# A hybrid decoder layer on one core: which expert's weights lie in the scratch's spare room

## The reference, cut to what matters

```python
logits = (xt @ w_router) + b_router
top_val, top_idx = lax.top_k(logits, 4)          # of 32 experts
gates = jax.nn.softmax(top_val, axis=-1)
hh = xb @ w_gu[e] + b_gu[e]                      # (tokens, 1024) @ (1024, 2048)
act = glu * jax.nn.sigmoid(1.702 * glu) * (lin + 1.0)
out += (act @ w_down[e] + b_down[e]) * gate      # (tokens, 1024) @ (1024, 1024)
```

## Time and profile before

| what | value |
|---|---|
| median of the runs | 1191.43 us |
| the profiled execution | 1193.07 us |
| its span, first to last instruction | 1191.3 us |
| around the span | 1.8 us |
| TensorE busy | 1137.9 us, 96% of the span |
| granted clock, mean | 0.997 |
| read from HBM | 433.04 MB |

### The profile page before, as it was taken

How to read it: one execution, slowest core, us unless ns; L and a number is a source line. 1 busy time by engine, 2 the same in 40 slices (tenths; PEclk the granted TensorE clock), 3 DMA queues, 4 the chain that set the end, 5 groups by cost and what they waited for, 6 DMA issues and landing times.

```text
span 1191.3 us, 16910 instructions
## 1 busy us (share of the span) xinstructions
PE 1137.9 (96%) x7060; PEld 482.3 (40%) x7060; DVE 282.8 (24%) x576; ACT 173.0 (15%) x319; POOL 0.2 (0%) x4
## 2 busy tenths in 40 slices
PE   7999999999999999999999999999999999999997
PEld 6888856533333333333333333333333333333234
DVE  2454734322111111112112111111111111111123
ACT  3323423110100000000100100000000000000015
POOL 0000000000000000000000000000000000000000
PEclk9999999999999999999999999999999999999999
DMA  9752026679899999999999999999999999999970
GB/s 367 328 212 74 30 116 239 247 298 415 348 418 427 429 426 429 430 429 427 430 428 427 430 429 427 430 429 427 429 429 427 428 430 427 429 429 427 429 329 35
DMA packets 34022, 434.67 MB, mean 365 GB/s; under 512 B 4032, under 2 KB 4288, under 8 KB 6976
## 3 DMA queue, kind: packets, MB, share of 16 engines
q1 hardware_dynamic: 33984, 434.11, 87.0%
HBM read 433.04 MB, written 1.05 MB: 364 GB/s over the span
## 4 chain that ended last, share of the span: by engine, by line
PE 44%; DMA 39%; DVE 1%; issue 0%; ACT 0%; SPq 0%; DVEq 0%
DMA ring<-in_we 38%; PE PS L909 30%; PE PS L1006 2%; PE PS L747 2%; PE PS L860 2%; PE PS L875 2%; PE PS L925 1%; PE PS L867 1%; PE PS L959 1%; DMA hT<-in_wproj 0%; PE PS L797 0%; PE PS L934 0%; PE PS L542 0%; PE PS L802 0%; PE PS L883 0%
## 5 line engine op out<-in xcount | busy, mean ns | idle before, releaser
L909 PE MATMUL PS<-ring,FV 128*64 128x512 f32 x2276 | 508.7, 596 | 22.6 <-DMA ring<-in_we 22.6
L909 PEld LDWEIGHTS PS<-ring,FV 128*64 128x64 f32 x2276 | 156.7, 137 | 355.4 <-issue 302.4
L909 PE MATMUL PS<-B,FV 128*64 128x512 f32 x772 | 175.1, 596 | 8.7 <-DMA B<-in_we 8.7
L909 PEld LDWEIGHTS PS<-B,FV 128*64 128x64 f32 x772 | 53.3, 137 | 115.6 <-issue 99.2
L530 PE MATMUL PS<-hT,ring 128*128 128x256 f32 x416 | 93.0, 382 | 1.0 <-ACT hT L1059 0.7
L530 PEld LDWEIGHTS PS<-hT,ring 128*128 128x128 f32 x416 | 78.3, 190 | 12.1 <-ACT hT L1059 0.9
L1540 DVE TENSOR_SCALAR rz<-con,lora 128x64 f32<-128x64 f32 x30 | 7.6, 255 | 304.5 <-PE PS L909 304.5
L1313 DVE TENSOR_TENSOR FV<-PS,prm 128x512 f32<-128x512 f32 x32 | 22.1, 692 | 184.4 <-PE PS L867 184.4
L1622 DVE TENSOR_SCALAR hT<-PS 128x512 f32<-128x512 f32 x32 | 22.1, 692 | 182.2 <-PE PS L909 182.2
L860 PE MATMUL PS<-xq,rz 128*64 128x512 f32 x256 | 62.0, 605 | 0.0
L1218 ACT ACTIVATE FV<-PS 128x512 f32<-128x512 f32 x32 | 19.1, 597 | 294.8 <-PE PS L959 294.8
(11 more groups left out here) (270 smaller groups left out, 686.2 us busy)
## 6 DMA issues: line engine op xcount, KB each, us to landing
ring<-in_we SPq DMA_DIRECT2D x135, 2048.0 KB, 23.4
B<-in_we SPq DMA_DIRECT2D x48, 2048.0 KB, 29.3
ring<-in_wz SPq DMA_DIRECT2D x7, 2048.0 KB, 23.2
ring<-in_we SPq DMA_DIRECT2D x14, 1024.0 KB, 7.3
ring<-in_wo SPq DMA_DIRECT2D x2, 2048.0 KB, 8.3
ring<-in_wgate SPq DMA_DIRECT2D x2, 2048.0 KB, 38.6
stash<-in_we SPq DMA_DIRECT2D x1, 2048.0 KB, 13.6
xq<-in_x SPq DMA_DIRECT2D x2, 512.0 KB, 6.0
```

The costliest lines, as they stand in the source:

```text
L909: mm = pe.matmul(PS[64 * h:64 * h + 64, bank_, :], lhs(4 * (q % 2) + k), early[u] if q == 0 and u < units else w[:, k, h, :], start=(first ...
```

## The change

The 14 units of scratch room take item 11's p1 and the first six units of item 11's p0 instead of item 3's. They are loaded at the same places in the attention part, from expert 11's weights. Item 3 is loaded in full by `ahead`, like its neighbours. In SP's order item 11's p0 is two units (512 KB) and its p1 is left out, and the wait and the two `wproj` DMAs come behind item 11's pieces, with the threshold 67 instead of 19. TensorE has item 11 written out, since it reads other rooms: items 0 to 3, a loop for items 4 to 9, items 10 and 11, a loop for items 12 to 29, and the last two. The kept piece has a semaphore of its own, so the thresholds of p1 change with it: `behind=True` marks the items after item 11, which wait for one landing of p1 less.

```diff
-        NEARLY, EARLY_ITEM = len(early), 3
+        NEARLY, KEPT_ITEM = len(early), 11
...
+        s_kept = sem("kept_item_second_piece_landed")
...
-            sp.dma_start(kept, t["we"][EARLY_ITEM, 1]).then_inc(s_we[1], 16)
+            sp.dma_start(kept, t["we"][KEPT_ITEM, 1]).then_inc(s_kept, 16)
...
-                sp.dma_start(dst, t["we"][EARLY_ITEM, 0, :, u * PW:(u + n) * PW]).then_inc(s_early, 16)
+                sp.dma_start(dst, t["we"][KEPT_ITEM, 0, :, u * PW:(u + n) * PW]).then_inc(s_early, 16)
...
-            def in_turn(i, odd, qs=range(6)):
+                    load(e if q < 3 else e_next, q, odd == (q < 3))
+
+            def in_turn(i, odd, qs=range(6), kept_item=False):
 
                 e = weights(i)
                 for q in qs:
+                    if kept_item and q == 1:
+                        continue
                     sp.wait_ge(s_used, 6 * i + (q - 5 if q < 3 else q - 11))
-                    load(e, q, odd)
+                    if kept_item and q == 0:
+                        sp.dma_start(ring[:, 0, NEARLY * PW:], t["we"][KEPT_ITEM, 0, :, NEARLY * PW:]).then_inc(s_we[0], 16)
+                    else:
+                        load(e, q, odd)
 
             ahead(2, False, halved=True)
-            ahead(EARLY_ITEM, True, rest=True)
-            sp.wait_ge(s_used, 6 * EARLY_ITEM + 1)
-            for k in range(2):
-                sp.dma_start(wproj1[k], t["wproj"][1, :, k * PW:(k + 1) * PW]).then_inc(s_ple1, 16)
+            ahead(3, True)
             with sp.Fori(1, EARLY) as p:
                 ahead(2 * p + 2, False)
                 ahead(2 * p + 3, True)
             in_turn(2 * EARLY + 2, False, range(3))
-            in_turn(2 * EARLY + 3, True)
+            in_turn(KEPT_ITEM, True, kept_item=True)
+            sp.wait_ge(s_used, 6 * KEPT_ITEM + 1)
+            for k in range(2):
+                sp.dma_start(wproj1[k], t["wproj"][1, :, k * PW:(k + 1) * PW]).then_inc(s_ple1, 16)
             with sp.Fori(EARLY, pairs) as p:
...
-            item(2, False, before=True)
-            item(EARLY_ITEM, True, units=NEARLY)
-            with pe.Fori(1, pairs) as p:
+            item(2, False)
+            item(3, True)
+            with pe.Fori(1, KEPT_ITEM // 2 - 1) as p:
                 item(2 * p + 2, False)
                 item(2 * p + 3, True)
-            item(2 * last_pair, False)
+            item(KEPT_ITEM - 1, False)
+            item(KEPT_ITEM, True, kept_item=True)
+            with pe.Fori(KEPT_ITEM // 2, pairs) as p:
+                item(2 * p + 2, False, behind=True)
+                item(2 * p + 3, True, behind=True)
+            item(2 * last_pair, False, behind=True)
             last_item = 2 * last_pair + 1
-            item(last_item, True, last=True)
+            item(last_item, True, last=True, behind=True)
```

More of the change, by code:

```diff
@@ L270, in fox_rwkv7_moe_ple @@
         s_odd = [sem(f"odd_expert_piece{q}_landed") for q in range(3, 6)]
-        s_early = sem("fourth_item_first_rows_landed")
+        s_early = sem("kept_item_first_rows_landed")
+        s_kept = sem("kept_item_second_piece_landed")
         s_ple = sem("layer_projection_landed")
@@ L431, in load, with ahead @@
                     .then_inc(landed(q, odd), 16)
-            def ahead(i, odd, rest=False, halved=False):
+            def ahead(i, odd, halved=False):
                 e, e_next = weights(i), weights(i, 1)
@@ L441, in ahead @@
                         continue
-                    if rest and q == 1:
-                        continue
                     sp.wait_ge(s_used, 6 * i + (q - 5))
[L445 to L448, removed]
-            def in_turn(i, odd, qs=range(6)):
+                    load(e if q < 3 else e_next, q, odd == (q < 3))
+            def in_turn(i, odd, qs=range(6), kept_item=False):
                 e = weights(i)
                 for q in qs:
+                    if kept_item and q == 1:
+                        continue
                     sp.wait_ge(s_used, 6 * i + (q - 5 if q < 3 else q - 11))
-                    load(e, q, odd)
+                    if kept_item and q == 0:
+                        sp.dma_start(ring[:, 0, NEARLY * PW:], t["we"][KEPT_ITEM, 0, :, NEARLY * PW:]).then_inc(s_we[0], 16)
+                    else:
+                        load(e, q, odd)
             ahead(2, False, halved=True)
-            ahead(EARLY_ITEM, True, rest=True)
-            sp.wait_ge(s_used, 6 * EARLY_ITEM + 1)
-            for k in range(2):
-                sp.dma_start(wproj1[k], t["wproj"][1, :, k * PW:(k + 1) * PW]).then_inc(s_ple1, 16)
+            ahead(3, True)
             with sp.Fori(1, EARLY) as p:
@@ L885, in scatter_last, with product @@
                     finish(mm, "tpe", f"s{b}")
-            def product(i, odd, q, bank_, lhs, first, units=0, before=False, halved=False, front=None):
+            def product(i, odd, q, bank_, lhs, first, kept_item=False, behind=False, halved=False, front=None):
                 weights = extra[q - 3] if odd and q >= 3 else ring[:, q, :]
-                if units and q == 1:
+                if kept_item and q == 1:
                     weights = kept
                 w = weights.rearrange("p (k h c) -> p k h c", k=4, h=2)
-                if units and q == 0:
+                units = NEARLY if kept_item and q == 0 else 0
+                if units:
                     pe.wait_ge(s_early, 16 * 5)
-                if before and q == 1:
-                    pe.wait_ge(s_we[1], 16 * i + 32)
+                if kept_item and q == 1:
+                    pe.wait_ge(s_kept, 16)
+                elif behind and q == 1:
+                    pe.wait_ge(s_we[1], 16 * i)
                 elif q < 3:
@@ L909, in product @@
                         mm = pe.matmul(PS[64 * h:64 * h + 64, bank_, :], lhs(4 * (q % 2) + k),
-                                       early[u] if q == 0 and u < units else w[:, k, h, :],
+                                       early[u] if u < units else w[:, k, h, :],
                                        start=(first and k == 0), stop=(q % 2 == 1 and k == 3))
@@ L917, in _, with item @@
             x_of, act_of = half_of(xT), half_of(aT)
-            def item(i, odd, first=False, last=False, units=0, before=False):
+            def item(i, odd, first=False, last=False, kept_item=False, behind=False):
                 pe.wait_ge(s_ohb, i + 1)
@@ L946, in item @@
                         former()
-                    product(i, odd, q, 6 + q // 2, x_of, False, units if q < 2 else 0, before, **halves(q))
+                    product(i, odd, q, 6 + q // 2, x_of, False, kept_item, behind, **halves(q))
                     if first and q < 3:
@@ L976, in _ @@
             pe.wait_ge(s_bt, 16)
-            item(0, False, first=True, before=True)
+            item(0, False, first=True)
             pe.wait_ge(s_dve, dve_at["tabs"])
             start_sums()
-            item(1, True, before=True)
+            item(1, True)
             pairs = pe.value_load(EI[0:1, NITEM + 2:NITEM + 3], min_val=NE // 2 - 2, max_val=NITEM // 2 - 2)
             last_pair = pairs + 1
-            item(2, False, before=True)
-            item(EARLY_ITEM, True, units=NEARLY)
-            with pe.Fori(1, pairs) as p:
+            item(2, False)
+            item(3, True)
+            with pe.Fori(1, KEPT_ITEM // 2 - 1) as p:
                 item(2 * p + 2, False)
                 item(2 * p + 3, True)
-            item(2 * last_pair, False)
+            item(KEPT_ITEM - 1, False)
[4 more added lines that the diff above has]
+            item(2 * last_pair, False, behind=True)
             last_item = 2 * last_pair + 1
-            item(last_item, True, last=True)
+            item(last_item, True, last=True, behind=True)
             pe.wait_ge(s_ysb, last_item + 1)
```

## The result

The changed kernel takes 1196.42 us (median of 9 runs, 1193.85 to 1197.76) beside 1192.59 us for the kernel before (9 runs on the same chip, 1189.94 to 1193.53). The ratio is 1.0031, with a 95% interval of 1.0022 to 1.0039: the change makes the kernel 3.7 us slower. The forecast was 2.0 us slower, 1193.4 us, with a range that ended at 1196.2; it started from 1191.43 us, the median of three runs, and the nine runs here have 1192.59. Executions with a mean granted clock of 0.998 or more are some 3 us shorter than those with 0.996 or 0.997 (of the kernel before beside e1 to e4, seven with a median of 1190.2 us against 22 with 1193.0), so where few runs are compared, the difference among the latter is given too. The profiled execution took 1196.42 us, its span is 1194.6 us, 3.3 us longer than before.

The account below looks back on a forecast made before the run. One saturated stream of weight pieces was taken to set the end, not TensorE. Stream gaps and savings (+0.7 us) and code fetches (+1.3 us) gave +2.0 us on 1191.4 us, so 1193.4 us, range 1190.6 to 1196.2 us.

Parts of the forecast that it names:

- the bound: From 343 us on, one stream of weight pieces at 428 GB/s sets the end; TensorE's own work doesn't.
- the gaps: Stream standing still: 5.4 us before item 11's p2, 0.6 us before the wproj halves, 0.6 us before item 12's p0.
- step 4: TensorE's longer code: about four more code fetches between 500 and 615, 0 to 1.4 us each, taken as 1.3 us in all.
- the range: Forecast time from 1190.6 us (no fetch slips, shorter gap, 1 us scatter) to 1196.2 us (three dear fetches and +0.7).
- Step 1: Item 3 loaded in full fills the slow stretch 311:343; item 4's p0 and everything behind it come 1.4 us late.
- Step 2: At item 11's p2, waiting for item 10's p2's room, the queue runs empty and the stream stands still 5.4 us.
- The rival (b): Whole stream: it stands still nowhere new, the 5.9 us of Step 1 are gained, 1185.5 us; chance 0.04.
- Step 3: At the wproj halves and item 12's p0: two stops of 0.6 us, bringing the sum so far to +0.7 us.
- three dear fetches: Code fetches beside the weight stream at the high price, 0.9 to 1.4 us each, assumed for the range's upper end.
- The rival (a): Added code fetches in the full stream cost 0.9 to 1.4 us each; slower, 1194.5 to 1197 us; chance 0.36.
- TensorE's branches: At the start of item 10 or 12, a TensorE stall on a taken branch would cost nothing.
- The fixed cost: Between a DMA's issue into an empty queue and its first data pass 2.7 us; the skill's figure is about 2.0 us.

Follow-up runs that it names:

- e1: The changed kernel run again with no edit; ratio to the kernel before 1.0033.
- e4: The changed kernel with item 11 loaded in full, its kept units fetched but never read; ratio to the kernel before 1.0040.
- e2: The changed kernel with SP issuing items 10 to 13 with the next item's p3 to p5 before that item's p0; 0.9971 of the kernel before, 1188.35 us.
- e6: The changed kernel with the two wproj halves issued behind item 13's pieces instead of before item 12's; ratio to the kernel before 1.0023.
- e5: The changed kernel with item 11's pieces issued in the order p0, p3, p4, p2, p5; ratio to the kernel before 1.0018.
- e10: The changed kernel with item 11's pieces issued as p0, p3, p4, p2, p5, a second run of e5; ratio to the kernel before 1.0017.
- e3: The kernel before with only TensorE's code changed: items 10 and 11 written out and a second loop; ratio 1.0013, +1.5 us.
- e7: The kernel before with items 4 to 19 written out in TensorE's program, sixteen more code fetches, no second loop; ratio 1.0028, +3.3 us.

## Why the prediction was wrong, step by step

The direction, the bound and the gaps held. Two steps failed: step 4 was mis-sized (slips by code fetches, put at 1.3 us for the four added fetches and at nothing for the others), and the top of the range left out the scatter of the starting value. The change came out at 3.7 us instead of 2.0, the time at 1196.4 us instead of 1193.4. Of these 3.0 us, 1.2 are the starting value (1192.59 us and not 1191.43) and 1.8 the change.

*Bound.* Right. Behind 700 the pair of 25.49 and 3.68 us goes on, and e2 and e4 move the time by what they do to the stream.

*Step 1, item 3 in full, +1.4 us.* Right: 311:343 runs at 429 GB/s, no wait of TensorE is new there, and from item 3's p5 to item 4's p0 the stream lost 1.7 us, 0.25 of it at one slip. The 0.3 us before that arise ahead of item 3.

*Step 2, the gap at item 11's p2, 5.4 us.* Right to 0.3 us in all three profiles of the changed kernel: 11.5, 11.8 and 11.5 us from item 10's p2 to item 11's, forecast 11.5 (7.6, 7.9 and 7.7 us from issue to landing). The rival (b), a gain of 5.9 us for want of a gap, is out.

*Step 3, `wproj` and item 12's p0, +0.7 us in the sum.* The stretch was 9.2 us and not 7.3. SP needed 557.69 - 555.50 = 2.2 us from the first half's issue to the piece's, not 1.9. The other 1.6 us are a late landing of item 12's p0 with the code fetch of 559.0 beside it; the forecast had that fetch in step 4.

*Step 4, the code fetches, 1.3 us: the mis-sized term.* The four added fetches were counted rightly (533, 559, 586 and 612). Beside them landings were late by 1.6 us (all at 559), 1.5 us (all at 558) and 2.2 us (1.0 at 558, 1.2 at 585) in the three profiles of the changed kernel, so they cost about 1.8 us there. Two things were overlooked. First, I had written that "the two gaps of steps 2 and 3 also swallow what falls into them". The fetch at 533 did cost nothing. But item 12's code is fetched at 558 to 559, where the stream has just started again, and in the three profiles and in e6 the piece took 9.2, 9.1, 8.6 and 9.1 us instead of 7.6. In e5 and e10, with a fetch at nearly the same time, it took 7.8 and 7.6, so it isn't a rule. Second, the forecast put at nothing the fetches that both kernels have. Behind 310 these cost 1.5, 2.0 and 0.7 us in the three profiles of the changed kernel (0.25 at 314, 1.0 at 391 and 0.2 at 1104; 1.5 at 313 and 0.5 at 1134; 0.7 at 391, where the next landing had made up 0.1), and 0.9 us behind 343 in the profile of the kernel before.

For the profiled pair the sum closes at the last wait of the chain: 0.7 (steps 1 to 3) + 0.3 (before item 3) + 0.3 (SP's issue) + 1.6 (added fetches) + 0.6 (the old ones, 1.5 less 0.9) = 3.5 us, against 3.4 in the table. Where the slips fall differs from profile to profile, and that the pair's 3.4 us lies so near to the 3.7 us of the medians is partly luck. The 1.5 us of e3 are no further term beside the slip at 559, since e3 has that fetch too. What stays open is why the fetches cost +1.5 us in e3's median while none of the four cost anything in e3's profile.

*The range.* Its top, 1196.2, is 1191.4 + 0.7 + three dear fetches. The lower end had 1 us for the scatter between medians of three, the top had nothing. From 1192.59 us the same top would have been 1197.4, with the measured 1196.42 inside; the range missed by 0.2 us for that reason.

*The rival (a)*, slower, 1194.5 to 1197, had 0.36. Its time is what came. Its mechanism, each of the four fetches at 0.9 to 1.4 us, is only half of it: one or two of the four were dear, and the rest is the starting value, SP and the older fetches.

*TensorE's branches.* Nothing: from 343 to 1100 e3 and e7 show no idle time of TensorE but its waits for pieces. The Trainium skill (Runtime: NRT & Kernel Launch, "Instruction fetch mechanics") calls the crossing of a block of code mostly hidden. For the engine that executes the code this case's traces agree. For the stream of weights they don't: +1.5 us in e3, +3.3 us in e7.

*The fixed cost.* The forecast worked with 2.7 us, the row, and not the about 2.0 us of the Trainium skill (DMA: Bandwidth & Descriptors, "Anatomy of one DMA"). That section gives its figure for DMAs issued through GpSimd, and those of this kernel are issued by SP; the prediction didn't say so. For a full piece the row was right. For a small DMA into an empty queue the measured value comes near the section's: in e10 the first 256 KB half landed 2.6 us after its issue, of which 0.6 us is transfer at 428 GB/s.

## What to carry to other kernels

Where one saturated stream sets the end, a saved transfer is worth only what the stream can do with the time: look which wait its next issue stands behind, and whether enough work is queued in front of that wait to cover the time from use to first data (here 3.9 + 2.7 us, more than one piece). Work taken out of a full queue needs room to run ahead, and the order of issue decides whether there is any; moving the same 14 units made the kernel 3.7 us slower in one order and 3.5 us faster in another. And code written out is not free when the stream of weights is already full: count the fetches, the old ones too where a change fills a stretch that used to stand still, and take 0.2 us (e7) to 0.4 us (e3) for each in the sum, with up to 1.6 us for a single one. Behind a gap the price can be the high one (1.0 to 1.6 us in four profiles of six, nothing in two). Last, give the scatter of the starting value to both ends of a range.

## What the runs showed of the hardware

- While 16 KB of code come in on the instruction queue, a landing of the full weight stream beside it is 0 to 1.6 us late. The landings behind it mostly follow 4.9 us apart again, so nearly all of the loss stays. Four more fetches cost 1.5 us (e3), sixteen 3.3 us (e7).
- The weight stream from HBM holds 428 to 429 GB/s over hundreds of microseconds on this core (before 343 to 1101; e7, with its sixteen fetches, 428).
- Between an issue into an empty queue and the landing pass 7.6 us for 2048 KB (item 11's p2 after the change) and 2.6 us for 256 KB (e10).
- Near 230 us, ahead of the experts, TensorE's granted clock falls to 1.2 GHz for a few microseconds in some executions: the mean over 200:250 is 0.97 in the profile before, 0.93 after and 1.00 in e7's. In all three TensorE had been busy without a break from 200 to 230. Where the clock stayed up, in e7, item 3's p5 landed 2.6 us sooner than before.
